# A stick-breaking attention whose softplus is split into a high and a low rounded part, with the mask added before the softplus and two copies moved one step later

## What is computed

```python
z = einsum(q, k) * scale                     # per head, 128 queries at a time
mask = kpos[None, :] < qpos[:, None]         # strictly causal
log_beta = log_sigmoid(z)
log_rem  = where(mask, log_beta - z, 0.0)    # = -softplus(z)
between  = cumsum(log_rem, reverse=True) - log_rem
w = where(mask, exp(log_beta + between), 0.0)
out = einsum(w, v)
```

## Time and profile before

| | us |
|---|---|
| median of 3 runs | 748.53 (748.49 to 749.07) |
| the profiled execution | 746.63 |
| its span in the trace | 744.8 |
| PE busy | 687.9 (92%) |
| DVE busy | 375.3 (50%) |
| ACT busy | 291.5 (39%) |

### The profile page before, as it was taken

The page is one execution under the profiler, slowest core; times in us unless marked ns, Lnnn a source line. Parts: engine busy times, 40 slices in busy tenths (PEclk is TensorE's granted clock), DMA queues, the critical chain, the costliest instruction groups (busy, mean ns, idle before and its releaser), DMA issues.

```text
span 744.8 us, 12414 instructions
## 1 busy us (share of the span) xinstructions
PE 687.9 (92%) x5172; PEld 514.5 (69%) x5172; DVE 375.3 (50%) x592; ACT 291.5 (39%) x427; POOL 55.0 (7%) x96
## 2 busy tenths in 40 slices
PE   4999999999978777778999999999999999999996
PEld 3897879654323122124999989998988888888885
DVE  3668861431110100104967986645876755665653
ACT  4245430341111010014676542669266543344532
POOL 0010000000000000001058740000000000000000
PEclk9999999999989888888999999999999999999999
DMA  9998999999999999999844434330554545664001
GB/s 372 424 423 365 371 413 425 425 403 427 426 425 428 428 426 426 426 424 427 349 192 161 180 141 168 147 114 8 220 201 167 211 143 213 225 226 169 2 0 57
DMA packets 29569, 208.11 MB, mean 279 GB/s; under 512 B 3267, under 2 KB 3523, under 8 KB 4677
## 3 DMA queue, kind: packets, MB, share of 16 engines
q1 hardware_dynamic: 29508, 207.26, 68.7%
HBM read 206.20 MB, written 1.05 MB: 278 GB/s over the span
## 4 chain that ended last, share of the span: by engine, by line
PE 75%; DMA 21%; DVE 1%; ACT 1%; issue 1%; SPq 0%; DVEq 0%
PE psum L423 74%; DMA raw<-in_w_exp 18%; DMA early<-in_w_ada_q 3%; PE psum L431 2%; DVE X L2500 0%; SPq L462 0%; ACT XT L2443 0%; DVE dT L1010 0%; ACT XB L859 0%; ACT G L1292 0%; DVE xn L1000 0%; DVE XB L2144 0%; DVE XT L1319 0%; ACT XB L1901 0%; SPq L465 0%
## 5 line engine op out<-in xcount | busy, mean ns | idle before, releaser
L423 PE MATMUL psum<-XB,whi 128*128 128x256 f32 (+1 forms) x1216 | 267.2, 309 | 2.4 <-DVE XB L661 1.9
L423 PEld LDWEIGHTS psum<-XB,whi 128*128 128x128 f32 x1216 | 197.4, 191 | 18.4 <-issue 2.9
L423 PE MATMUL psum<-XB,wlo 128*128 128x256 f32 x736 | 207.5, 282 | 0.0
L503 DVE TENSOR_TENSOR wlo<-raw,whi 128x2048 fp32r<-128x2048 f32 (+1 forms) x88 | 168.8, 1958 | 31.4 <-ACT whi L486 31.4
L486 ACT ACTIVATE whi<-raw 128x2048 fp32r<-128x2048 f32 (+1 forms) x79 | 139.0, 1800 | 47.6 <-PE psum L423 34.1
L423 PEld LDWEIGHTS psum<-XB,wlo 128*128 128x128 f32 x736 | 140.3, 191 | 0.2
L423 PE MATMUL psum<-raw,G 128*32 128x512 f32 x448 | 62.6, 681 | 16.4 <-DMA raw<-in_w_exp 8.5
L423 PEld LDWEIGHTS psum<-raw,G 128*32 128x32 f32 x448 | 14.1, 117 | 59.0 <-issue 37.5
L423 PE MATMUL psum<-whi,FH 128*128 128x512 f32 (+1 forms) x132 | 50.7, 384 | 0.0
L423 PE MATMUL psum<-whi,FL 128*128 128x512 f32 (+1 forms) x132 | 50.6, 384 | 0.0
L423 PE MATMUL psum<-wlo,FH 128*128 128x512 f32 (+1 forms) x132 | 50.6, 383 | 0.0
(11 more groups left out here) (373 smaller groups left out, 819.1 us busy)
## 6 DMA issues: line engine op xcount, KB each, us to landing
raw<-in_w_exp SPq DMA_DIRECT2D x85, 1024.0 KB, 24.8
raw<-in_w_ff SPq DMA_DIRECT2D x32, 1024.0 KB, 5.3
raw<-in_w_in SPq DMA_DIRECT2D x22, 1024.0 KB, 7.0
raw<-in_w_ada SPq DMA_DIRECT2D x13, 1024.0 KB, 11.9
raw<-in_w_in_t SPq DMA_DIRECT2D x8, 1024.0 KB, 19.2
X<-in_w_exp SPq DMA_DIRECT2D x5, 1024.0 KB, 26.4
raw<-in_w_out_t SPq DMA_DIRECT2D x4, 1024.0 KB, 12.1
rawx<-in_w_exp SPq DMA_DIRECT2D x4, 1024.0 KB, 22.4
```

The lines of the kernel that those rows point to most:

```text
L423: return e.matmul(o, l, r, start=start, stop=stop, skip_group_check=True)
L503: e.tensor_tensor(wlo[j % NS][:, x], ring[slot[i]][:, x], whi[j % NS][:, x], ALU.subtract).then_inc(*steps_(("lo", j, x.start // 1024), *[ ...
```

## The change

UI and NON become fp32r tiles; UI is now made on DVE. A new tile zp of 1536 columns holds, for two heads in turn, the softplus rounded to fp32r (`zh`) and the rest (`zl`). The mask is added to the logits in PSUM before ACT reads them; the product with 0 and 1 and the later masking fall away. The sum products run twice, on the high and on the low part, each as UI against 384 and NON against 128 columns. On ACT the logits of head 7 come after the exponential of head 5, and the copies for XH 0 and 1 (and DVE's XL 0 and 1) come one step later.

```diff
@@ act_hybrid
             for i in range(1, 10):
-                if i < 7:
+                if i < 6:
                     act_z(e, i + 1)
                 if i <= 8:
                     h = i - 1
-                    e.wait_ge(*at(("w_masked", h)))
+                    e.wait_ge(*at(("w", h)))
...
+                if i == 6:
+                    act_z(e, i + 1)
                 act_pieces(e, SB_HIGH[i])
...
-                if i == 5:
+                if i == 6:
                     e.wait_ge(*at("sb_first"))
                     e.activation(XH[:, 0, :], sbq[:, 0, :], ACT.Copy).then_inc(*hyb_act(("cat2H", 0)))
-                if i in (5, 7, 9):
-                    c = i // 2 - 1
+                if i in (6, 7, 9):
+                    c = 1 if i == 6 else i // 2 - 1
@@ act_z
-            e.wait_ge(*at(("z", h)))
+            e.wait_ge(*at(("z_masked", h)))
             if h >= 3:
-                e.wait_ge(*at(("w", h - 3)))
+                e.wait_ge(*at(("z_soft", h - 3)))
@@ dve_hybrid
                 else:
-                    dve_z(e, 0)
-                    dve_z(e, 1)
+                    for h in range(2):
+                        dve_masked(e, h)
+                    for h in range(2):
+                        dve_z(e, h)
                 if hd == 3:
                     dve_pieces(e, 153)
-                    dve_masked(e, 0)
...
             for i in range(1, 10):
-                if 2 <= i <= 8:
-                    dve_masked(e, i - 1)
                 if i < 7:
+                    dve_masked(e, i + 1)
                     dve_z(e, i + 1)
@@ dve_masked
-            e.wait_ge(*at(("w", h)))
+            e.wait_ge(*at(("z", h)))
@@ dve_z
+            if h >= 2:
+                e.wait_ge(*at(("w", h - 2)))
             e.wait_ge(*hyb_dve.last())
-            d = z.rearrange("p (a b) -> p a b", a=3)[:, 0:3:2, :]
-            e.tensor_tensor(d, d, row2(C["su"]), ALU.mult).then_inc(*hyb_dve(("z_soft", h)))
+            e.tensor_copy(zh[h % 2], z).then_inc(*hyb_dve())
+            e.wait_ge(*hyb_dve.last())
+            e.tensor_tensor(zl[h % 2], z, zh[h % 2], ALU.subtract).then_inc(*hyb_dve(("z_soft", h)))
@@ pe_hybrid
-                    mm(e, p[:, 0:256], UI[:, :], z[:, 0:256], False, False)
-                    mm(e, p[:, 128:256], NON, z[:, 256:384], False, False)
-                    mm(e, p[:, 256:384], UI[:, :], z[:, 256:384], False, True).then_inc(*hyb_pe(("w", h)))
+                    for z in (zh[h % 2], zl[h % 2]):
+                        mm(e, p[:, 0:384], UI[:, :], z[:, 0:384], False, False)
+                        x = mm(e, p[:, 128:256], NON, z[:, 256:384], False, z is zl[h % 2])
+                    x.then_inc(*hyb_pe(("w", h)))
```

More of the change, by code:

```diff
@@ L141, in build @@
         raw += [sb(f"raw{NR + 2 * NS + i}", [128, 2048]) for i in range(2)]
+        halves = ExitStack()
+        zp = tensors(halves)("zp", [128, 1536], fr)
+        halves.close()
         XT = sb("XT", [128, 8, 256])
@@ L267, in build @@
         zs = [tmpB[:, 0:384], tmpB[:, 512:896]]
-        NON = ta("non", [128, 128])[:, :]
+        NON = ta("non", [128, 128], fr)[:, :]
+        zh = [zp[:, 384 * k:384 * k + 384] for k in range(2)]
+        zl = [zp[:, 768 + 384 * k:1152 + 384 * k] for k in range(2)]
         RQ = ta("rqrow", [128, 256])[:, :]
-        UI = ta("ui", [128, 128])
+        UI = ta("ui", [128, 128], fr)
         NEGST = ta("negst", [128, 128])
@@ L1735, in pool_hybrid @@
             e.memset(RESET[:, 0:256:64], 0.0).then_inc(*hyb_pool("reset"))
-            e.tensor_scalar(UI[:, :], C["su"], 1.0, None, ALU.subtract).then_inc(*hyb_pool("ui"))
+            e.tensor_scalar(NEGST[:, :], C["su"], 1.0, None, ALU.subtract).then_inc(*hyb_pool())
             e.wait_ge(*hyb_pool.last())
-            e.tensor_scalar(NEGST[:, :], UI[:, :], 1e30, None, ALU.mult).then_inc(*hyb_pool("negst"))
+            e.tensor_scalar(NEGST[:, :], NEGST[:, :], 1e30, None, ALU.mult).then_inc(*hyb_pool("negst"))
             pool_decays(e, 0)
@@ L2001, in dve_hybrid @@
             e.tensor_scalar(NON, ones[:, :], -1.0, None, ALU.mult).then_inc(*hyb_dve("non"))
+            e.tensor_scalar(UI[:, :], C["su"], 1.0, None, ALU.subtract).then_inc(*hyb_dve("ui"))
             dve_pieces(e, 138)
@@ L2129, in dve_masked @@
             d = bank(("z", h))[:, 0:384].rearrange("p (a b) -> p a b", a=3)[:, 0:3:2, :]
-            e.wait_ge(*at(("w", h)))
+            e.wait_ge(*at(("z", h)))
             if h == 0:
                 e.wait_ge(*at("negst"))
-            e.tensor_tensor(d, d, row2(NEGST[:, :]), ALU.add).then_inc(*hyb_dve(("w_masked", h)))
+            e.tensor_tensor(d, d, row2(NEGST[:, :]), ALU.add).then_inc(*hyb_dve(("z_masked", h)))
         def dve_weigh(e, n):
@@ L2268, in pe_hybrid @@
                     h = i - 1
-                    p, z = bank(("z", h)), zt[h % 3]
-                    e.wait_ge(*at(("z_soft", h)))
+                    p = bank(("z", h))
                     e.wait_ge(*at("non"))
                     e.wait_ge(*at("ui"))
-                    mm(e, p[:, 0:256], UI[:, :], z[:, 0:256], False, False)
-                    mm(e, p[:, 128:256], NON, z[:, 256:384], False, False)
-                    mm(e, p[:, 256:384], UI[:, :], z[:, 256:384], False, True).then_inc(*hyb_pe(("w", h)))
+                    e.wait_ge(*at(("z_soft", h)))
+                    for z in (zh[h % 2], zl[h % 2]):
+                        mm(e, p[:, 0:384], UI[:, :], z[:, 0:384], False, False)
+                        x = mm(e, p[:, 128:256], NON, z[:, 256:384], False, z is zl[h % 2])
+                    x.then_inc(*hyb_pe(("w", h)))
                 if i == 9:
```

## The result

| us | before | changed | ratio |
|---|---|---|---|
| first comparison, 9 runs each | 748.49 | 751.40 | 1.0037 [1.0025, 1.0050] |
| second, on another occasion | 748.32 | 749.62 | 1.0012 [0.9999, 1.0025] |
| third | 748.58 | 749.88 | 1.0015 [1.0005, 1.0024] |
| profiled execution (first) | 746.63 | 751.03 | |
| its span | 744.8 | 749.2 | |

The forecast was 748.8, that is +0.3. The changed kernel is slower, by 1.3 to 2.9 us according to the comparison; the interval of the second just includes no change. Medians are over all runs; ratios and intervals are taken without the few runs that lie over 1.5% above their kernel's fastest, and are not quotients of these medians.

What follows compares the result with a forecast made beforehand. PE's own products and waits were taken to bound the stretch. 2.08 - 3x - 0.59 - x + 0.1 = 1.59 - 4x, +0.3 us with x = 0.32, gave 748.8 us; range 746.7 to 751.2.

Steps and rivals of the forecast that it cites:

- The first place: Step 2: PE's logits of head 3 wait for ACT's exponential of head 0, behind DVE's masking of head 2: +2.08 us.
- The sum products: PE's sum block of one head, now with fp32r operands: 0.58 us instead of 0.90.
- x: Time saved per head in PE's sum block: 0.32 us, with ends at 0.08 and 0.40.
- The assumed parts of 0.18 and 0.10: Prices in us given to one fp32r product in the sum block: 0.18 for 384 columns, 0.10 for 128.
- The eight products of 36 columns: Earlier profile rows, eight from 133.20 to 134.01, 0.10 us apart, from which the short fp32r product was priced at 0.10.
- The second place: Steps 5 to 7: exponential of head 5 stands right behind the table load, so PE's values of heads 4, 5 come -0.59 us.
- The moved copies: Step 8's product needs a bank that the later subtraction XL 1 frees: a wait of 0 to 0.2 us, taken as 0.1.
- step 8: Its product takes the bank of the values of heads 2 and 3; forecast to start within 0.2 us of its release.
- the first rival: Clock falls in the new wait at step 2, place G comes 2.3 us later: 751.1 us; chance 0.14.

Runs made afterwards that it cites:

- the kernel with the split alone: Kernel before with the softplus going into the sums in two rounded parts, order and masking untouched: 747.14 against 748.58, ratio 0.9986.
- the eighteen products: Changed kernel plus 18 products nobody reads in PE's list ahead of the logits of head 3: ratios to the kernel before 1.0010 and, repeated, 1.0010.
- the nine products: Changed kernel plus 9 products nobody reads in PE's list ahead of the logits of head 3: ratio to the kernel before 1.0014.
- the last kernel: Changed kernel, exponentials of heads 0 and 3 before ACT's passes of heads 2 and 5, DVE's masking of head 6 before gated-state subtraction: 745.26 against 747.94, ratio 0.9968.
- the order without the split: Changed kernel's order with the sum products in plain f32, without high and low part: ratios to the kernel before 1.0025 and 1.0046.

## Why the prediction was wrong

- **The first place: right.** +2.08 forecast, +2.12 measured, by the links named; PE idle 2.35 us of 2.4.
- **The sum products: right in sum.** x = 0.32 per head: four times 0.32 in the kernel with the split alone. The assumed parts of 0.18 and 0.10 were not what the block showed. That the block of head 7 takes the forecast 0.58 us is in part luck: it follows products with weights and had taken 0.80 before, so it saved 0.22, while the 0.90 is that of a block right behind logits, and such a block takes 0.63 now (474.77 to 475.40 in the changed kernel). The eight products of 36 columns were eight instructions, that is four plain f32 products; 0.10 us was a price for one instruction.
- **The second place: right.** -0.57 for -0.59.
- **The moved copies:** the wait of 0.1 us at step 8 did not come. It and the smaller saving of head 7 cancel, by luck: -0.20 for -0.22.
- **The step that failed: the clock, taken to stay at 1.00.** The sum of +0.3 had no term for it; it stood in the first rival, with 0.14. "After a pause of 1.89 us between dense products the clock stayed" was the argument against. It was one row, far from this place, and the wait here was longer. What the runs showed in its place: with 2.35 us the clock fell to 0.50 in three profiles of three, with 2.04 in one of two, with 1.80 elsewhere in one of one, and the fall cost 1.50 us behind the wait. The rival should have carried more than half of the chance. Its price, though, was too high: its 2.3 us came from a stretch that ran 5.93 us at a mean of 0.55, while here three stretches of 2 us had 0.72, 0.50 and 0.92.

The first rival, wait with clock, is thus what happened in the profiles: the forecast sum with the measured fall gives 0.3 + 1.5 = 1.8 us over the kernel before, between the +1.3 of two comparisons and the +2.9 of the first. In the parts of the profile that the forecast had terms for, 2.66 - 0.57 - 0.20 = 1.89; the 0.35 of the final norm, for which it had none, comes on top. With the fall taken out, by the eighteen products, the same parts give 1.15 - 0.57 - 0.20 = +0.38, next to the forecast of +0.3.

The Trainium skill, "TensorE: Matmul & The Clock Gate", section "What's actually happening", makes the low level the default that activity lifts. The trace agrees: at the same lateness, 1.00 where PE worked through 2.3 us of it, 0.50 where it stood.

**What stays open:** how often the clock falls in executions without a profile. Runs show one mean clock each, from 0.955 to 0.974 for the changed kernel, over the whole span, and a fall of a few microseconds in 750 is lost in it. By medians, filling the wait gave back 0.4 us, not 1.5, which would fit a fall in some of the executions only, but this is argued and not shown. Why the first comparison lost 2.9 us and the later two 1.3 is open for the same reason, and some 0.8 of those 2.9 us (1.8 and the 0.35 of the final norm taken off) have no cause here. Nor is it known why the final norm is longer.

## What to carry to other kernels

When a reordering puts a standstill of some two microseconds or more into the densest engine, price it twice: its length, and what the clock may take behind it. An operation that frees a buffer (here the exponential of head h) belongs ahead of operations on the same engine that wait for a busy neighbour (here the passes of head h+2, behind DVE's masking): that one move made the loss a gain. And time saved on PE ahead of a wait that others end only lengthens the wait: 1.80 us for 1.03 in the kernel with the split alone.

## What the hardware showed unexpectedly

- The clock fell from 2.4 to 1.2 GHz after a single pause amid dense products: 1.80 us (one profile of one), 2.04 (one of two), 2.35 (three of three). It stayed after 1.20 to 1.27 us (the changed kernel's second place, the nine products, the last kernel) and after 1.03. The 1.89 us of the earlier trace rows left it at 1.00, and in the first profile of the order without the split the same early place stood for 2.25 us and kept 1.00 behind it, so the pause's length alone does not decide near 2 us:

```profile
17.14 0.50 PE L428 MATMUL psum<-XB,whi 128*128 128x256 f32 x2 [2.25 <-DVE XB L666]
```

```profile
18.00:20.00 2.00, 2.00 (x20) 2.00 (x18) 2.00 (x4) 1.55 (x3) 0.00 (x0) 1.00 1.00 422
```

- It fell not in the pause but after PE had begun again: in the changed kernel 482 to 484 still has 1.00 with PE standing most of it, and 486 to 488 has 0.50 with PE busy throughout. Each fall cost 1.5 us (8.88 against 7.35, 9.22 against 7.67, and 5.28 against 3.78).
- In head 7's block the fp32r products of 128 columns were followed after 0.06 and 0.12 us, those of 384 columns after 0.17 and 0.23, alternating, 0.58 us in all. Right behind logits, the first of 384 columns took 0.28 (474.77 to 475.05 in the changed kernel).
